# The inverse of a chunked delta rule: its 32x32 diagonal blocks in compact form and in 32x32 array tiles

## The reference, cut to what matters

```python
l_mat = jnp.einsum('nbhid,nbhjd->nbhij', kb, kc) * decay_strict
eye = jnp.eye(A_CHUNK, dtype=jnp.float32)
rhs = jnp.concatenate([vc * bc[..., None], kb * jnp.exp(gcum)[..., None]], axis=-1)
sol = lax.linalg.triangular_solve(eye + l_mat, rhs, left_side=True, lower=True, unit_diagonal=True)
...
def step(s, xs):
    v_new = u_n - jnp.einsum('bhcd,bhde->bhce', w_n, s)
    o_n = jnp.einsum('bhcd,bhde->bhce', qd_n, s) + jnp.einsum('bhij,bhje->bhie', a_n, v_new)
    s = s * gl_n[..., None, None] + jnp.einsum('bhcd,bhce->bhde', kd_n, v_new)
```

## Time and profile before

| | us |
|---|---|
| median of 3 runs | 2233.93 |
| lowest, highest | 2231.27, 2236.58 |
| span of the profiled execution | 2233.1 |
| TensorE busy | 2155.3 (97%) |
| VectorE busy | 982.5 (44%) |
| ScalarE busy | 633.1 (28%) |
| GpSimd busy | 143.8 (6%) |

### The profile page before, as it was taken

One profiled execution on the slowest core, in us unless ns is written; L12 is line 12 of the kernel. 1 busy time (PEld: TensorE's weight loads), 2 busy tenths in 40 slices (PEclk: granted clock), 3 DMA queues, 4 the chain that ended last, 5 costly groups with the idle time before them and its releaser, 6 DMA issues.

```text
span 2233.1 us, 28302 instructions
## 1 busy us (share of the span) xinstructions
PE 2155.3 (97%) x12000; PEld 1683.8 (75%) x12000; DVE 982.5 (44%) x1762; ACT 633.1 (28%) x1085; POOL 143.8 (6%) x181
## 2 busy tenths in 40 slices
PE   7999999999999999999999999999999999999997
PEld 2248888887788888888888888888873345888886
DVE  1334334554245555545554565362245333454333
ACT  3222321232322222322223212542244332222121
POOL 0000000000011111100011001100000002010000
PEclk9999999999999999999999999999999999999999
DMA  8752112222221111211111211444322332444332
GB/s 305 275 199 66 57 57 62 67 89 62 67 75 58 48 57 58 67 49 57 57 48 58 65 53 54 130 143 130 104 76 89 109 132 94 151 145 176 121 114 85
DMA packets 151927, 218.29 MB, mean 98 GB/s; under 512 B 9632, under 2 KB 99993, under 8 KB 150521
## 3 DMA queue, kind: packets, MB, share of 16 engines
q1 hardware_dynamic: 136777, 173.08, 24.8%
q0 software_dynamic: 7248, 29.25, 3.8%
q10 hardware_dynamic: 7776, 14.16, 1.8%
HBM read 198.11 MB, written 18.35 MB: 97 GB/s over the span
## 4 chain that ended last, share of the span: by engine, by line
PE 87%; DVE 4%; ACT 4%; DMA 2%; issue 1%; POOL 0%; SPq 0%; ACTq 0%; POOLq 0%; DVEq 0%
PE psum L1324 20%; PE psum L1326 20%; PE psum L1325 20%; PE psum L1410 6%; PE psum L1377 4%; PE psum L1375 3%; PE psum L1557 2%; ACT inv L601 1%; PE psum L1387 1%; PE psum L1385 1%; PE psum L1352 1%; DMA w_raw<-w_mod_dram 1%; PE psum L1393 1%; ACT square_out L633 1%; DVE inv L929 1%
## 5 line engine op out<-in xcount | busy, mean ns | idle before, releaser
L845 DVE TENSOR_TENSOR w_lo<-w_raw,w_hi 128x1024 fp32r<-128x1024 f32 (+1 forms) x233 | 284.9, 1223 | 654.2 <-ACT w_hi L535 653.9
L535 ACT ACTIVATE w_hi<-w_raw 128x1024 fp32r<-128x1024 f32 (+1 forms) x233 | 246.3, 1057 | 1129.4 <-PE psum L1326 1101.7
L1324 PE MATMUL psum<-h_hi,w_hi 128*128 128x512 f32 (+1 forms) x1168 | 486.4, 416 | 5.7 <-DVE w_lo L845 3.5
L1325 PE MATMUL psum<-h_lo,w_hi 128*128 128x512 f32 (+1 forms) x1168 | 461.3, 395 | 0.0
L1326 PE MATMUL psum<-h_hi,w_lo 128*128 128x512 f32 (+1 forms) x1168 | 461.0, 395 | 0.0
L1326 PEld LDWEIGHTS psum<-h_hi,w_lo 128*128 128x128 f32 (+1 forms) x1168 | 220.4, 189 | 50.9
L1324 PEld LDWEIGHTS psum<-h_hi,w_hi 128*128 128x128 f32 (+1 forms) x1168 | 220.8, 189 | 44.4 <-DVE w_lo L845 4.9
L1325 PEld LDWEIGHTS psum<-h_lo,w_hi 128*128 128x128 f32 (+1 forms) x1168 | 221.3, 189 | 33.7
L1410 PE MATMUL psum<-w_raw_mod,silu_c 128*2 128x512 f32 x256 | 114.0, 600 | 1.3 <-ACT silu_c L660 0.8
L1375 PEld LDWEIGHTS psum<-invT,L 128*128 128x128 f32 x768 | 93.6, 192 | 22.0 <-DVE inv L929 19.0
L1375 PE MATMUL psum<-invT,L 128*128 128x64 f32 x768 | 95.3, 274 | 12.3 <-DVE inv L929 11.4
(11 more groups left out here) (293 smaller groups left out, 3106.8 us busy)
## 6 DMA issues: line engine op xcount, KB each, us to landing
...
```

The source lines that it names most:

```text
L535: act.activation(part(whi[i % 2], p), part(place, p), ACT.Copy).then_inc(S("w_hi"), 1)
L845: dve.tensor_tensor(part(wlo[i % 2], p), part(raw_of(n)[0], p), part(whi[i % 2], p).bitcast(f32), ALU.subtract).then_inc(S("w_lo"), 1)
L1324: pe.matmul(out_ap, lh, rh, start=first, stop=False, skip_group_check=shared)
L1325: pe.matmul(out_ap, lh, rl, start=False, stop=False, skip_group_check=shared)
```

## The change

The 32x32 diagonal blocks are kept in a compact form: YC (transposed inverse) and XC (inverse) have 128 partitions x 4 heads x 32 columns, one 32x32 block per group of 32 partitions. For n = 0 to 4 each matmul of 128x128 becomes four of 32x32 (q), block by block in its own tile of the array: 32 matmuls per slot, on 32 columns (n = 0, where L is multiplied with the identity) or 16. The masks shrink to 32 and 16 columns, and VectorE's operations to 128 and 64 elements per partition; its transposes are of 128 elements per partition.

For n = 5, couple and correct read YC and XC; correct has four more matmuls per direction, which give the transposed product as well, and VectorE writes it to X64. The flip slot goes, and its ScalarE copy. GpSimd copies the diagonal blocks from YC to YY (four per direction) and from XC to X64 (two per direction) when correct4 is done; TensorE waits for them (diag) before couple6 and correct6. What was subtracted in YY for n = 5 and 6 is now written, times -1; YY and X64 are set to zero once, at the start. at is written to resid (RR) instead of YY, and stands behind z.

```diff
-IDENT, LE, GE, GT, LT_, ONES, STAGE = 0, 128, 256, 384, 512, 640, 768
+IDENT, LE, GE, GT, LT_, ONES, EYE32, PAIR2, STAGE = 0, 128, 256, 384, 512, 640, 768, 800, 864
 BLOCKS = [1, 2, 4, 8, 16, 32, 64]
-MASKED = BLOCKS[:-2]
-NCONST = STAGE + len(MASKED) * 2 * 64
+MASKED = BLOCKS[1:-2]
+NCONST = STAGE + len(MASKED) * 2 * 16
...
+    r, j = (a % 32)[:, None], np.arange(32)[None, :]
+    parts.append(r == j)
+    for backward in (0, 1):
+        parts.append((r // 2 == j // 2) & (j == r + (-1 if backward else 1)))
...
+            cols = np.arange(32)[(np.arange(32) // s) % 2 == (0 if backward else 1)]
             want = cols // s + (1 if backward else -1)
-            parts.append(block[:, None] == want[None, :])
+            parts.append(r // s == want[None, :])
...
-                kinds += [("couple", n)] + [("correct", n)] * (n > 0) + [("flip", n)] * (n == len(BLOCKS) - 2)
-            kinds += [("at", 0)] * lat + [("kt", 0)] * (not last) + [("ks", 0)] * (not early) + [("z", 0)]
-            kinds += [("qs", 0), ("az", 0)] * lat + [("kz", 0)] * (not last)
+                kinds += [("couple", n)] + [("correct", n)] * (n > 0)
+            kinds += [("kt", 0)] * (not last) + [("ks", 0)] * (not early) + [("z", 0)]
+            kinds += [("at", 0), ("qs", 0), ("az", 0)] * lat + [("kz", 0)] * (not last)
...
+    YC = [at(f"inv32T{b}", [P, 4, 32], A_C + 30720 + 1024 * b) for b in (0, 1)]
+    XC = [at(f"inv32{b}", [P, 4, 32], A_C + 31232 + 1024 * b) for b in (0, 1)]
+    X64 = at("inv64", [P, 4, 64], A_X64)
...
+        def other32(b):
+            return PS[:, b * 512 + 128:b * 512 + 256].rearrange("p (u n) -> p u n", u=4)
...
+                    for d in (0, 1):
+                        pool.memset(YY[d][:], 0.0).then_inc(S("inv_zero"), 1)
+                    pool.memset(X64[:], 0.0).then_inc(S("inv_zero"), 1)
                     pool.wait_ge(S("kv_spill"), 16 * NT)
                     pool.memset(SS[:], 0.0).then_inc(S("states0"), 1)
+                    pool.wait_ge(S("inv_zero"), 3)
...
+                for d in (0, 1):
+                    pool.wait_ge(S(f"gd{d}"), [s["i"] for s in SLOTS if s["pair"] == pi and s["kind"] == "correct"
+                                               and s["n"] == len(BLOCKS) - 3][0] + 1)
+                    for q in range(4):
+                        pool.tensor_copy(YY[d][32 * q:32 * q + 32, :, 32 * q:32 * q + 32], YC[d][32 * q:32 * q + 32]).then_inc(
+                            S(f"diag{d}"), 1)
+                    for q in (2 * d, 2 * d + 1):
+                        c = 32 * (q % 2)
+                        pool.tensor_copy(X64[32 * q:32 * q + 32, :, c:c + 32], XC[d][32 * q:32 * q + 32]).then_inc(
+                            S(f"diag{d}"), 1)
+                for d in (0, 1):
+                    pool.wait_ge(S(f"diag{d}"), 6 * (pi + 1))
...
                     elif k == "at":
-                        act.activation(YY[d][:], ps, ACT.Copy).then_inc(done, 1)
+                        act.activation(RR[d][:], ps, ACT.Copy).then_inc(done, 1)
...
-                return dve.transpose(XX[d][:].rearrange("p u n -> p (u n)"), YY[d][:].rearrange("p u n -> p (u n)"))
+                return dve.transpose(XC[d][:].rearrange("p u n -> p (u n)"), YC[d][:].rearrange("p u n -> p (u n)"))
...
-                        mo = STAGE + (2 * n + d) * 64
-                        mask = consts[:, mo:mo + 64].unsqueeze(1).to_broadcast([P, 4, 64])
                         if n == 0:
-
-                            upd = 0 if d else 1
-                            y_of = lambda e: YY[d][:].rearrange("p u (b e s) -> p u b e s", e=2, s=1)[:, :, :, e, :]
-                            i_of = lambda e: odd1(ident, 1, d, e).unsqueeze(1).to_broadcast([P, 4, 64, 1])
-                            dve.tensor_copy(y_of(1 - upd), i_of(1 - upd))
-                            src = ps.rearrange("p u (b e) -> p u b e", e=2)[:, :, :, 0 if d else 1]
-                        else:
-                            src = bank4(b, 64)
-                        ins = dve.tensor_tensor(PM[d][:], src, mask, ALU.mult)
-                        if n > 0:
-                            ins.then_inc(done, 1)
+                            mask = consts[:, PAIR2 + 32 * d:PAIR2 + 32 * d + 32].unsqueeze(1).to_broadcast([P, 4, 32])
+                            eye = consts[:, EYE32:EYE32 + 32].unsqueeze(1).to_broadcast([P, 4, 32])
+                            ln(dve.tensor_tensor(YC[d][:], bank4(b, 32), mask, ALU.mult))
+                            ln(dve.tensor_tensor(YC[d][:], eye, YC[d][:], ALU.subtract))
+                            flip_blocks(d).then_inc(done, 1)
                             continue
-                        ln(ins)
-                        ln(dve.tensor_tensor(y_of(upd), i_of(upd), PM[d][:].unsqueeze(3), ALU.subtract))
-                        flip_blocks(d).then_inc(done, 1)
+                        mo = STAGE + (2 * (n - 1) + d) * 16
+                        mask = consts[:, mo:mo + 16].unsqueeze(1).to_broadcast([P, 4, 16])
+                        dve.tensor_tensor(PM[d][:, :, 0:16], bank4(b, 16), mask, ALU.mult).then_inc(done, 1)
...
-                            yv = YY[d][r0:r0 + 64, :, c0:c0 + 64]
-                            dve.tensor_tensor(yv, yv, bank4(b, 64)[r0:r0 + 64], ALU.subtract).then_inc(S(f"gy{d}"), 1)
+                            dve.tensor_scalar(YY[d][r0:r0 + 64, :, c0:c0 + 64], bank4(b, 64)[r0:r0 + 64], -1.0, None,
+                                              ALU.mult).then_inc(S(f"gy{d}"), 1)
                             continue
                         if n == len(BLOCKS) - 2:
+                            if slot["pair"] == 0:
+                                dve.wait_ge(S("inv_zero"), 3)
                             for c0, r0 in HALF_BLOCKS[d]:
-                                yv = YY[d][c0:c0 + 32, :, r0:r0 + 32]
-                                ins = dve.tensor_tensor(yv, yv, bank4(b, 32)[c0:c0 + 32], ALU.subtract)
-                            ins.then_inc(done, 1)
+                                dve.tensor_scalar(YY[d][c0:c0 + 32, :, r0:r0 + 32], bank4(b, 32)[c0:c0 + 32], -1.0, None, ALU.mult)
+                            c0, r0 = HALF_BLOCKS[d][d]
+                            dve.tensor_scalar(X64[r0:r0 + 32, :, c0 % 64:c0 % 64 + 32], other32(b)[r0:r0 + 32], -1.0, None,
+                                              ALU.mult).then_inc(done, 1)
                             continue
-                        yv = odd(YY[d][:], BLOCKS[n], d)
-                        pv = bank4(b, 64).rearrange("p u (b s) -> p u b s", s=BLOCKS[n])
+                        yv = odd(YC[d][:], BLOCKS[n], d)
+                        pv = bank4(b, 16).rearrange("p u (b s) -> p u b s", s=BLOCKS[n])
                         ln(dve.tensor_tensor(yv, yv, pv, ALU.subtract))
                         flip_blocks(d).then_inc(done, 1)
...
+                    if k == "couple" and n == LASTB or k == "correct" and n == LASTB:
+                        pe.wait_ge(S(f"diag{d}"), 6 * (slot["pair"] + 1))
...
-                            ins = pe.matmul(bank4(b, 64)[c0:c0 + 64, u, :], XX[d][c0:c0 + 64, u, c0:c0 + 64],
+                            ins = pe.matmul(bank4(b, 64)[c0:c0 + 64, u, :], X64[c0:c0 + 64, u, :],
                                             PM[d][c0:c0 + 64, u, :], start=True, stop=True)
-                        elif k in ("couple", "correct") and n == LASTB - 1:
+                        elif k == "couple" and n == LASTB - 1:
 
                             for c0, r0 in HALF_BLOCKS[d]:
-                                lhs, rhs = ((LL[d][r0:r0 + 32, u, c0:c0 + 32], YY[d][r0:r0 + 32, u, r0:r0 + 32]) if k == "couple"
-                                            else (XX[d][c0:c0 + 32, u, c0:c0 + 32], PM[d][c0:c0 + 32, u, 0:32]))
-                                ins = pe.matmul(bank4(b, 32)[c0:c0 + 32, u, :], lhs, rhs, start=True, stop=True)
-                        elif k == "couple" and n == 0:
-                            ins = pe.transpose(ps[:, u, :], LL[d][:, u, :], ident)
+                                ins = pe.matmul(bank4(b, 32)[c0:c0 + 32, u, :], LL[d][r0:r0 + 32, u, c0:c0 + 32],
+                                                YC[d][r0:r0 + 32, u, :], start=True, stop=True)
+                        elif k == "correct" and n == LASTB - 1:
+
+                            for c0, r0 in HALF_BLOCKS[d]:
+                                ins = pe.matmul(bank4(b, 32)[c0:c0 + 32, u, :], XC[d][c0:c0 + 32, u, :],
+                                                PM[d][c0:c0 + 32, u, 0:32], start=True, stop=True)
+                            c0, r0 = HALF_BLOCKS[d][d]
+                            ins = pe.matmul(other32(b)[r0:r0 + 32, u, :], PM[d][c0:c0 + 32, u, 0:32],
+                                            XC[d][c0:c0 + 32, u, :], start=True, stop=True)
                         elif k == "couple":
-                            rhs = odd1(YY[d][:, u, :], BLOCKS[n], d)
```

(18 more changed lines are left out.)

11 lines of the change are left out of this document (3 added, 8 removed).

## The result

The median of the changed kernel is 2123.6 us (four runs, 2122.8 to 2127.6), of the kernel before on the same chip 2235.3 us: a ratio of 0.9493 [0.9472, 0.9514]. The change makes the kernel 5.1% faster. The profiled spans are 2121.6 us after and 2233.1 us before, 111.5 us apart, where 121.2 was forecast.

The account below looks back on a forecast made before the run. TensorE, busy for 97% of the span, was taken as the bound. Savings of 91.2 + 10.9 - 1.2 + 11.8 (waits) + 8.5 (clock) = 121.2 us from 2233.9 gave 2113 us, range 2094 to 2170.

Parts of the forecast that it names:

- The pace of four tiles: Slots of sizes 2 to 16: four tiles work at once, period 2.22 us instead of 3.17, 96 slots save 91.2 us.
- The waits behind slot 0 and the low clock: Behind slot 0: shorter VectorE work saves 11.8 us of TensorE waits, and fewer half-clock stretches save 8.5 us.
- The flip: The slot of 8 transposes in each pair goes: 0.91 us x 12 = 10.9 us saved.
- Slot 0: First slot of each pair: 64 records replace 8 transposes, 2.22 against 2.25 us, counted as nothing.
- the slots of size 32: Correction of size 32: 8 more matmuls per slot in a third tile, costing 0.1 us x 12 = 1.2 us.
- The copies: GpSimd's 12 copies per pair before the size-64 coupling: 0.35 us each, hidden up to 0.48 us each.
- rival 2: GpSimd's copies end the wait before size 64: +26 us, 2139 us, more if the clock falls; chance 0.15.
- VectorE off the path: In the corrections, VectorE's drop from 1.1 to 0.6 us per direction gains no time itself; TensorE returns 1.4 us later.
- 1 (fewer tiles): Small slots: fewer than four tiles at once or a fixed issue pace, 2145 or 2163 us; chance 0.22.
- 4 (a floor per start): Small slots: starts never closer than 25 ns, 64 records take 1.60 us, 2232 us, no change; chance 0.03.
- 3 (the feed): Small-tile periods: instruction supply can't feed TensorE, at 55 ns per record +178 us, 2291 us; chance 0.07.
- 5 (the clock): Stage of small tiles: the clock falls, a third of it at 1.2 GHz gives +58, 2171 us; chance 0.08.

Follow-up runs that it names:

- slot0_long: The changed kernel with transposes of 512 and 256 elements more on VectorE per direction, in slot 0 alone: 2158.0 us, ratio 0.9642.
- double_copies: The changed kernel with 24 GpSimd copies per pair instead of 12, the added ones into a dead buffer, TensorE waiting for all: 2186.6 us, ratio 0.9774.
- vector_long: The changed kernel with one more VectorE transpose of 128x384 elements per direction in the four masked corrections: 2125.0 us, ratio 0.9507.
- phase2: The changed kernel with the scan started two steps later among the gate matmuls, the program otherwise the same: 2119.4 us in its one run.
- beta_phase: The changed kernel with ScalarE's beta scaling moved from inverse to residual, in portions within small corrections, and the scan shifted by two steps: 2107.6 us, ratio 0.9417.
- probe: The changed kernel with seven bursts of 32x32 matmuls behind TensorE's last work; only the pace counted: 32 ns per record in one tile, 8.2 in four.

## Why the prediction was right, and where it was off

**The pace of four tiles** (91.2 us) was right. By slot (from the last gate matmul before it to the first behind it, less one gate step of 0.23 us) a small slot of before costs 1.70 us and of after 0.75, over 96 slots 91.2 us. The period was put at 2.22 and is 2.25; the difference lies in the gate matmuls behind the slot, see below. The step of 31 ns per tile, read from five records, is 32 in the burst of 96, and "nothing in it is shared by two tiles but not by four" held down to one PSUM bank. By the Trainium skill's rule on PSUM banks (TensorEngine Tiling (Array Packing), section Gotcha 1: PSUM Pressure), set aside ahead, a slot would have had 1.98 us; the trace disagrees with 0.73.

**The waits behind slot 0 and the low clock** (11.8 and 8.5 us) were right in cause and too low. All slots of L1375 and L1377 cost 186.3 us before, 23.1 over 96 x 1.70; those of L1404 and L1408 cost 74.7 after, 2.7 over 96 x 0.75, of which 2.5 are waits for issue that had no term. Before, 7 of the groups of six gate matmuls took over 2.0 us where the median, first start to last, is 1.24: 6.3 us in all, none after. None of the seven stretches at clock 0.50 is left among the slots; a new one stands behind them at 1365 us, after the wait of 2.89 us shown above (1.7). So 23.1 + 6.3 - 2.7 - 1.7 = 25.0 us were won and not 20.3. There was more to win than reckoned: "1.2 us lost, once per pair" was read in a latent pair, and the first four pairs, over the context, lose 2.1 us each (752.01 to 756.05 in before, less 1.93):

```profile
753.30 1.11 PE L1375 MATMUL psum<-invT,L 128*128 128x64 f32 x8 [0.89 <-DVE inv L929]
755.13 1.11 PE L1375 MATMUL psum<-invT,L 128*128 128x64 f32 x8 [0.73 <-DVE inv L929]
```

The 2.6 us that should have stayed behind slot 0 are one wait of 0.2, and of the 3.4 us of low clock nothing stayed there. slot0_long shows the cause from the other side: waits back, clock down.

**The flip** gave 10.7 us (10.9): 9.5 in its slot and 1.2 in the gate matmuls behind it, whose second start comes 0.31 us after the first and not 0.23. **Slot 0** gave 0.3 (0), and **the slots of size 32** cost 0.6 us more (1.2). The terms of the sum together: 91.2 + 25.0 + 10.7 + 0.3 - 0.6 = 126.6 us, where 121.2 stood.

**The copies** are hidden, as said. They take 4.1 us in five of the 12 pairs, 0.35 us from start to start, as taken, and 5.0 to 5.1 in the seven where one of them met w_lo (2.21 against 1.32 us for four). What was priced too low here is what happens beyond the cover: rival 2's "more if the clock falls behind it" had no figure, and in double_copies the clock and what it slows cost 27 us beside the 36 of waiting.

**VectorE off the path** in the corrections was right (vector_long, 1.4 us).

**What has no term is the shortfall**: 126.6 - 111.5 = 15.1 us. Four parts make it up:

- 4.0 us: behind a small slot a group of six gate matmuls takes 1.275 us from first start to last where it took 1.238 (means), 37 ns in each of 96, and behind slot 0 32 ns in each of 12. Some 24 of the 37 are in the first step: 0.34 us (903.71 to 904.05) and not 0.32 (1039.91 to 1040.23). "Six gate matmuls at their pace of 0.23 us" had no step for the return from small tiles.
- 6.8 us: slots whose matmuls the change leaves as they are wait where they did not before. By kind, z 21.0 to 23.7 us, the Gram products 20.4 to 23.65, az 13.6 to 14.7, couplings of size 64 +1.0, decay and qs +0.3 each, corrections of size 64 +0.1, against kt and at together 25.0 to 23.1.
- 1.5 us: the wait for w_lo behind the scan, 2.89 us where it was 1.41.
- 2.9 us outside the middle window, where both kernels do the same work. They are of the size of the scatter: over the kernels profiled here with the same work there, the part ahead takes 620.9 to 625.4 us and the part behind 566.2 to 572.3. Behind the scan after has two stretches at clock 0.50 (1583.5 and 1767.9 us) and before one (1692.0), which is 1.7 us.

The step that failed is the one on VectorE: "that gains no time itself, since TensorE is back only 1.4 us later". It is true for the corrections, but I looked at TensorE's new neighbours alone, and not at where each w_lo would fall in the shorter periods and beside which GpSimd operation. For 4.4 of the 6.8 us the trace names this cause. Gram waits in four slots, 0.81 us in each, every time behind a w_lo of 2.21 us, and az in two, 0.55 us in each, behind one of 1.82:

```profile
885.11 1.16 PE L1371 MATMUL psum<-kT_latent 128*128 128x128 f32 x8 [0.41 <-DVE resid L1014]
```

This row follows the w_lo of 881.81 above. In phase2 and in beta_phase there are two and one of these waits, again each behind a long w_lo. The 2.7 us of z are another thing: no w_lo near its long slots takes over 1.23 us, and where the trace names what z waits for, it is ScalarE's scaling, its copy of kt or VectorE's resid, in the new order of the slots. That the collision itself makes the waits is argued from these rows: no kernel ran without the overlap in the same phase.

**The rivals.** 1 (fewer tiles) and 4 (a floor per start) fell in the probe: 8.2 ns per record for four tiles, 32 for one. 2 (GpSimd) did not happen, with 0.7 us to spare in the tightest pair, and appears at 24 copies. 3 (the feed) did not happen, at 4.1 us per 256 instructions against a limit of 3.5 to 4.0, and appears with twice the matmuls at +210 us, the low clock included. Its price per record (55 ns) was too high: the probe has 3.5 us / 128 = 27 ns. 5 (the clock) did not happen, no stretch at 0.50 lies among the slots of after; its mechanism exists (probe, 2108.60 to 2112.00), where few full-size matmuls stand between the small ones. In the scan six stand between any two slots.
